# Conditioning units in the gaps of three norms, and the order of work around six norms, in a one-core decoder step

## What is computed

```
m = silu(c) @ W_ada + b_ada                 # per layer: 9 x 1024 outputs, for 9 conditioning vectors
shift1, scale1, gate1, shiftM, scaleM, gateM, shift2, scale2, gate2 = split(m, 9)
adaLN(x)  = rmsnorm(x) * g * (1 + scale) + shift
ffn(x)    = x + 0.5 * gate * ((silu(a) * b) @ W2),  a, b = split(adaLN(x) @ W1)
layer:  x = ffn1(x);  x = x + gateM * Mixer(adaLN(x));  x = ffn2(x)
```

## Time and profile before

| what | value |
|---|---|
| median of 3 runs | 1674.65 us (1674.52 to 1679.98) |
| profiled execution | 1671.24 us |
| its span in the trace | 1669.6 us (1.6 us lie around it) |
| PE busy | 1548.7 us (93%) |
| DVE, ACT, POOL busy | 871.4, 706.4, 252.2 us |
| granted PE clock, mean | 0.958 of full speed |

### The profile page before, as it was taken

The page is one execution under the profiler, slowest core; times in us unless marked ns, Lnnn a source line. Parts: engine busy times, 40 slices in busy tenths (PEclk is TensorE's granted clock), DMA queues, the critical chain, the costliest instruction groups (busy, mean ns, idle before and its releaser), DMA issues.

```text
span 1669.6 us, 32114 instructions
## 1 busy us (share of the span) xinstructions
PE 1548.7 (93%) x12092; PEld 1423.8 (85%) x12092; DVE 871.4 (52%) x1263; ACT 706.4 (42%) x896; POOL 252.2 (15%) x370
## 2 busy tenths in 40 slices
PE   5999999899899999899999899999988778899996
PEld 2899988887799998799999797899966557799996
DVE  1644443696644444544444632687457776644442
ACT  3433333432533333433333433566456784433332
POOL 2600000681400000100001101122230430100000
PEclk9899999999999999999999998899889898999998
DMA  9966678440676668776665552344571563654452
GB/s 294 262 226 226 210 253 271 144 131 15 192 248 220 219 221 267 230 239 221 222 186 155 159 160 63 89 114 125 218 240 52 173 202 122 194 184 159 146 165 87
DMA packets 269006, 304.80 MB, mean 183 GB/s; under 512 B 9945, under 2 KB 257857, under 8 KB 268792
## 3 DMA queue, kind: packets, MB, share of 16 engines
q1 hardware_dynamic: 260304, 274.96, 52.4%
q0 software_dynamic: 8624, 28.77, 5.3%
HBM read 300.51 MB, written 11.92 MB: 187 GB/s over the span
## 4 chain that ended last, share of the span: by engine, by line
PE 79%; DVE 6%; DMA 6%; ACT 6%; issue 2%; POOL 0%; SPq 0%; ACTq 0%; DVEq 0%; POOLq 0%
PE ps L2017 12%; PE ps L2018 11%; PE ps L2021 11%; PE ps L1998 7%; PE ps L1999 7%; PE ps L2000 7%; DMA raw<-in_ffn_w_dram 5%; PE ps L2031 3%; PE ps L2276 2%; PE ps L2278 2%; PE ps L2277 2%; PE ps L2254 2%; DVE wL L1304 2%; ACT wH L851 1%; PE ps L2117 1%
## 5 line engine op out<-in xcount | busy, mean ns | idle before, releaser
L1304 DVE TENSOR_TENSOR wL<-raw,wH 128x2048 fp32r<-128x2048 f32 (+2 forms) x176 | 366.7, 2083 | 392.7 <-ACT wH L851 392.5
L851 ACT ACTIVATE wH<-raw 128x2048 fp32r<-128x2048 f32 (+2 forms) x176 | 306.2, 1740 | 592.8 <-PE ps L2021 288.3
L1998 PE MATMUL ps<-hH,wL 128*128 128x288 f32 x848 | 260.9, 308 | 24.1 <-POOL hL L657 21.8
L2017 PE MATMUL ps<-hL,wH 128*128 128x288 f32 x976 | 267.5, 303 | 2.3 <-DVE hL L1920 1.8
L2018 PE MATMUL ps<-hH,wH 128*128 128x288 f32 x976 | 263.4, 296 | 0.0
L2000 PE MATMUL ps<-hH,wH 128*128 128x288 f32 x848 | 255.4, 301 | 0.0
L1999 PE MATMUL ps<-hL,wH 128*128 128x288 f32 x848 | 255.3, 301 | 0.0
L2017 PEld LDWEIGHTS ps<-hL,wH 128*128 128x128 f32 x976 | 184.3, 189 | 18.0 <-issue 16.0
L2017 PE MATMUL ps<-hidL,wH 128*128 128x288 f32 x704 | 194.7, 304 | 3.0 <-ACT wH L851 3.0
L2018 PE MATMUL ps<-hidH,wH 128*128 128x288 f32 x704 | 191.1, 297 | 0.0
L1998 PEld LDWEIGHTS ps<-hH,wL 128*128 128x128 f32 x848 | 165.1, 195 | 27.1 <-issue 24.3
(11 more groups left out here) (414 smaller groups left out, 2318.6 us busy)
## 6 DMA issues: line engine op xcount, KB each, us to landing
raw<-in_ffn_w_dram SPq DMA_DIRECT2D x88, 1024.0 KB, 5.2
ada<-in_ada_w_dram SPq DMA_DIRECT2D x72, 1024.0 KB, 5.2
raw<-in_ffn_w_dram SPq DMA_DIRECT2D x32, 768.0 KB, 4.7
raw<-in_ffn_w_dram SPq DMA_DIRECT2D x32, 640.0 KB, 5.3
craw<-in_cache_cmp_kv_dram SPq DMA_DIRECT2D x64, 256.0 KB, 3.6
raw<-in_nsa_w_in_dram SPq DMA_DIRECT2D x10, 1024.0 KB, 5.4
raw<-in_even_w_in_dram SPq DMA_DIRECT2D x8, 1024.0 KB, 5.5
kvp<-in_cache_sel_kv_dram POOLq DMA_DIRECT2D x64, 128.0 KB, 3.2
```

Source lines behind the costliest of these rows:

```text
L851: nc.scalar.activation(wH[parity][:, 0:k * UW], raw[parity][:, 0:k * UW], ACT.Copy).then_inc(hi_done, 1)
L1304: nc.vector.tensor_tensor(wL[parity][:, 0:k * UW], raw[parity][:, 0:k * UW], wH[parity][:, 0:k * UW].bitcast(F32), ALU.subtract).then_inc( ...
L1998: nc.tensor.matmul(o, l_, rhsH, start=first, stop=False)
L2017: nc.tensor.matmul(ps[:, banks + t, 0:T], wH[parity][:, c:c + P], L[:, k, :], start=first and k == k0, stop=False)
```

## The change

- Norms 2, 3 and 5 get two conditioning units each (32, 33; 56, 57; 68, 69), norm 0 keeps one (8). The first one of a pair is multiplied and turned in the gap, and finished by DVE after the norm's fourth chunk; the second one is multiplied right behind the turn. Its own turn comes in the first iteration of the W1 loop.
- The W1 loops have 11, 10, 10 and 2 units instead of 11, 11, 11 and 4. The turn of a unit comes one weight unit later than before: behind the next iteration's first unit, the last one behind the loop.
- SP sends both units of a norm between the first two loads of W1. In f = 3 it waits ahead of them for the last split of the attention output instead of the last output unit's end.
- The 2 MB of `w1c` go out in four pieces, each ahead of a quarter of W2.
- In every norm ACT rounds the sample columns first, ahead of chunk 0, without waiting for it.
- At the end of f = 0 and f = 2 DVE makes `wL` of the next stage's first unit ahead of the last update of x.
- The two loads of `c` move from POOL's queue to the head of SP's, and the constant fill no longer covers their rows.

```
-        ADA_IN_W1 = [9, 33, 57, 68]
-        ADA_PER_W1 = [HALF_PAIRS, HALF_PAIRS, HALF_PAIRS, 4]
+        ADA_IN_W1 = [9, 34, 58, 70]
+        ADA_PER_W1 = [HALF_PAIRS, HALF_PAIRS - 1, HALF_PAIRS - 1, 2]
+ADA_AT_NORM = [(8,), (), (32, 33), (56, 57), (), (68, 69)]
+        for pair in ADA_AT_NORM[2], ADA_AT_NORM[3], ADA_AT_NORM[5]:
+            ada_slot[pair[0]] = 1
...
 SP
+            sp.dma_start(rows[0:KD, 4, :], a["c_prompt"]...)          # from POOL, ahead of const
+            sp.dma_start(rows[KD:KD * NC, 4, :], a["c_sample"]...)
                 send(base, 0, w1v[f][:, :, 0:UW], KD)
-                if f < 3:
-                    send_one(a1 - 1)
+                if f == 3:
+                    sp.wait_ge(o_split, 3)
+                for n in ADA_AT_NORM[NORM_OF[f]]:
+                    send_one(n)
                 send(base + 1, 1, w1v[f][:, :, DFF:DFF + UW], KD)
-                if f == 3:
-                    sp.wait_ge(unit_used, OUT1 + 6)
                 send_one(a1)
...
                 if f == 2:
-                    quarter(0)
                     sp.wait_ge(ada_used, ADA_BY_NORM[4])
-                    for v in range(2):
-                        sp.dma_start(w1c[:, v, :, :], ...).then_inc(w1_landed, 16)
+                    for q in range(4):
+                        v, c = q // 2, q % 2 * 8
+                        sp.dma_start(w1c[:, v, c:c + 8, :], ...).then_inc(w1_landed, 16)
+                        quarter(q)
...
 POOL, norm
-                pool.wait_ge(hhi_done, 9 * k + 2)
+                pool.wait_ge(hhi_done, 9 * k + 1)
...
 ACT, norm
-                if ADA_AFTER_NORM[k] is not None:
-                    take_ada(ADA_AFTER_NORM[k])
+                if len(ADA_AT_NORM[k]) == 2:
+                    take_ada(ADA_AT_NORM[k][0])
+                act.wait_ge(ys_ready, 4 * k + 3)
+                nc.scalar.activation(hH[:, :, NP_:T], tmp[:, :, NP_:T], ACT.Copy).then_inc(hhi_done, 1)
                 for c in range(KD):
                     ...
-                    if c == 0:
-                        act.wait_ge(ys_ready, 4 * k + 3)
-                        nc.scalar.activation(hH[:, :, NP_:T], tmp[:, :, NP_:T], ACT.Copy).then_inc(hhi_done, 1)
+                if ADA_AT_NORM[k]:
+                    take_ada(ADA_AT_NORM[k][-1])
                 split(SECOND[k], 1)
...
 DVE, norm and ffn
-                    dve.wait_ge(hhi_done, 9 * k + (c + 2 if c else 1))
+                    dve.wait_ge(hhi_done, 9 * k + c + 2)
+                    if c == 3 and len(ADA_AT_NORM[k]) == 2:
+                        finish_ada(ADA_AT_NORM[k][0], link)
-                        finish_ada(a1 + j, ln)
+                        finish_ada(a1 + j - 1, ln)
+                finish_ada(a1 + ADA_PER_W1[f] - 1, link)
+                        if last and u == 2 and f in (0, 2):
+                            lower(n + 4, 0)
                         if u == (2 if last else 3):
                             pair_update(NORM_OF[f], q, bank, n + 3, ln)
-                        if not last or u < 2 or f < 3 and u == 2:
+                        if not last or u < 2 or f == 1 and u == 2:
...
 PE
+                for t, n in enumerate(ADA_AT_NORM[k]):
                     ada_unit(n, ada_slot[n], count[n])
-                    turn_ada(n)
+                    if t == 0 and len(ADA_AT_NORM[k]) == 2:
+                        turn_ada(n)
...
                     unit(na, 0, 0, 0, KD, hH, hL, True, True, NORM_OF[f])
                     if conditioned:
+                        turn_ada(a1 + j - 1)
                         ada_unit(a1 + j, 0, count[a1] + 16 * j)
                     pe.wait_ge(h_done, J + 1)
                     unit(na + 1, 1, 2, 0, KD, hH, hL, True, True)
-                    if conditioned:
-                        turn_ada(a1 + j)
+                turn_ada(a1 + ADA_PER_W1[f] - 1)                       # behind the loop
```

More of the change, by code:

```diff
@@ L485, in _ @@
         def _(sp):
+            sp.dma_start(rows[0:KD, 4, :], a["c_prompt"].rearrange("b (c p) -> (b c) p", p=P)).then_inc(c_landed, 16)
+            sp.dma_start(rows[KD:KD * NC, 4, :], a["c_sample"].rearrange("b (c p) -> (b c) p", p=P)).then_inc(c_landed, 16)
             sp.dma_start(const[:, :], a["consts"]).then_inc(const_landed, 16)
@@ L536, in ffn @@
                 if f == 2:
-                    quarter(0)
                     sp.wait_ge(ada_used, ADA_BY_NORM[4])
-                    for v in range(2):
-                        sp.dma_start(w1c[:, v, :, :], a["cmp_w1"][0, v].rearrange("(c p) h -> p c h", p=P)).then_inc(w1_landed, 16)
-                with sp.Fori(1 if f == 2 else 0, 4) as q:
-                    quarter(q)
+                    for q in range(4):
+                        v, c = q // 2, q % 2 * 8
+                        sp.dma_start(w1c[:, v, c:c + 8, :], a["cmp_w1"][0, v].rearrange("(c p) h -> p c h", p=P)[:, c:c + 8, :]).then_inc(w1_landed, 16)
+                        quarter(q)
+                else:
+                    with sp.Fori(0, 4) as q:
+                        quarter(q)
             def startup():
@@ L779, in _ @@
             pool.memset(cT[:, :, :], 0.0).then_inc(ones_ready, 1)
-            pool.memset(rows[:, :, :], 0.0).then_inc(ones_ready, 1)
+            pool.memset(rows[:, 0:4, :], 0.0).then_inc(ones_ready, 1)
             pool.wait_ge(ones_ready, 3)
-            pool.dma_start(rows[0:KD, 4, :], a["c_prompt"].rearrange("b (c p) -> (b c) p", p=P)).then_inc(c_landed, 16)
-            pool.dma_start(rows[KD:KD * NC, 4, :], a["c_sample"].rearrange("b (c p) -> (b c) p", p=P)).then_inc(c_landed, 16)
             flat = a["ada_b"].rearrange("l (c p) -> (l c) p", p=P)
@@ L1007, in odd @@
                 act.wait_ge(unit_used, OUT1 + 2)
-                act.wait_ge(w1_landed, 32)
+                act.wait_ge(w1_landed, 64)
                 for v in range(2):
@@ L1381, in norm @@
                     ins.then_inc(y_whole, 1)
-                if ADA_AFTER_NORM[k] is not None:
-                    finish_ada(ADA_AFTER_NORM[k], link)
             def ffn(f):
@@ L2058, in sum_squares @@
                 last_pair(k)
-                n = ADA_AFTER_NORM[k]
-                if n is not None and k > 0:
+                for t, n in enumerate(ADA_AT_NORM[k]):
                     ada_unit(n, ada_slot[n], count[n])
-                    turn_ada(n)
+                    if t == 0 and len(ADA_AT_NORM[k]) == 2:
+                        turn_ada(n)
             def ffn(f):
@@ L2224, in odd @@
                 pe.wait_ge(pe_copied, 1)
-                pe.wait_ge(w1_landed, 32)
+                pe.wait_ge(w1_landed, 64)
                 for v in range(2):
@@ L2643, in _ @@
                     pe.wait_ge(x_ready, KD)
-                    sum_squares(0, True)
+                    folded(0)
+                    last_pair(0)
             ada_unit(ADA_FIRST, ada_slot[ADA_FIRST], count[ADA_FIRST])
-            turn_ada(ADA_FIRST)
             ffn(0)
@@ L2692 @@
 SECOND = [1, IN0 + 1, FFN01 + 1, FFN10 + 1, IN1 + 1, FFN11 + 1]
-ADA_AFTER_NORM = [8, None, 32, 56, None, None]
+ADA_AT_NORM = [(8,), (), (32, 33), (56, 57), (), (68, 69)]
 _OUTS = [(1, 256, 1024), (8, 4, 1024), (1, 256, 1, 2, 4, 64), (8, 4, 1, 2, 4, 64), (1, 256, 1, 2, 4, 64), (8, 4, 1, 2, 4, 64),
```

## The result

The changed kernel takes 1687.7 us (median of 6 runs, 1685.94 to 1690.19), the kernel before 1674.6 beside it: a ratio of 1.0081 (95% interval 1.0064 to 1.0098). It is slower by 13 us, where 16.5 us of gain were forecast; the time lies above the range. The profiled execution took 1690.19 us, with a span of 1688.4, 18.8 longer than before.

The account below looks back on a forecast made before the run. PE was taken as the bound, busy 1548.7 of 1669.6 us. Terms -4.3 - 5.4 - 1.0 + 0.1 - 1.6 - 4.3 + 0 = -16.5 from the median 1674.65 gave 1658 us, range 1651 to 1667.

Parts of the forecast that it names:

- Units out of the W1 loops: W1 loops: fewer conditioning products and turns, moved turns wait for nothing; -4.28 us.
- the slower one: Rival, W1 loops: weights fall behind and conditioned iterations grow; 1684 at 1.2 us each; chance 0.05.
- the clock in the gaps: Gaps of norms 2, 3 and 5: second product keeps the clock at 1.00, low stretches go; -5.4 us.
- The clock falls anyway: Rival, gaps of norms 2, 3 and 5: clock drops all the same, 5.4 becomes 1.5; 1662; chance 0.20.
- the rival in which the clock stays up in norms 1 and 4 too: Shorter gaps there also keep the clock up, 2.1 + 1.7 us more gain; 1654.4; chance 0.08.
- The loops: W1 loops: iterations take 14.19 us with a conditioning unit and 12.77 without.
- ACT's order: Norms: samples rounded first start PE 0.5 us earlier; -1.0 counted in norms 1 and 4, +0.1 in norm 0.
- not under 15: Sign, norms: PE's wait for POOL's `hL` should fall from 21.8 us to under 15.
- the full doubling that the prediction weighed as its other end: Norms: DVE's first remainder doubles beside POOL; five starts 0.5 us later, sum 1.0 less.
- `lower` ahead of the update: Ends of f = 0 and f = 2: L1333 comes 0.87 and 0.7 us earlier; -1.57 together, at worst nothing.
- `w1c` in pieces: W2 of f = 2: PE's 2.98 us wait and its low-clock stretch go; -4.3 us, at the other end 0.
- The start: Program start: `c` earlier, other loads later; taken as 0, between -1.0 and +0.8; third unit not after 18.7.

Follow-up runs that it names:

- One: Changed kernel with one edit: in the W1 loops DVE finishes the previous iteration's conditioning unit ahead of `th`; 1661.3 us, ratio 0.9914.
- Four: One with the two loads of `c` back in POOL's queue; 1659.8 us, ratio 0.9911.
- Six: One with a single conditioning unit instead of two in norms 2 and 5, the pair kept in norm 3; 1662.5 us, ratio 0.9937.
- Three: Changed kernel with the two loads of `c` back in POOL's queue; 1691.9 us, ratio 1.0087.
- Seven: One with `w1c` whole again, in two loads of 1 MB behind the first quarter of W2; 1665.3 us, ratio 0.994.
- Ten: One with ACT's order in the norm undone, chunk 0 rounded ahead of the samples; 1660.5 us, ratio 0.992.
- Eleven: One with `lower` behind the last update of x again in f = 0 and f = 2; 1661.6 us, ratio 0.9923.
- Two: Kernel before with only the turns one weight unit later, and one conditioning unit in norm 5's gap; 1699.1 us, ratio 1.0143.
- Five: One with a single conditioning unit instead of two in each of norms 2, 3 and 5; 1671.3 us, ratio 0.9981.
- Eight: One with idle matmuls, whose results nothing reads, filling the gaps of norms 1 to 5; 1655.4 us, ratio 0.9875.
- Nine: Eight with the two loads of `c` back in POOL's queue; 1654.0 us, ratio 0.9886.

## Why the prediction was wrong

**The step that failed first** is "*Units out of the W1 loops*": "The moved turns wait for nothing: the copy and the bias of the unit before lie one weight unit back, some 6 us. DVE's `finish_ada` comes later by the same amount and runs as often." It was worked out for the middle of a loop and holds there, by only 1.36 us (586.40 to 587.76): DVE's chain behind a unit takes about 5 of the 6.4 us that it has. For the turn behind the loop there is no unit in between: the prediction counted these four turns, but gave them no wait. They wait 21.0 us, the clock behind them costs about 7.8, and both come back when the part alone is put into the kernel before. None of the rivals named it; the slower one (weights late in the W1 loops) did not happen: iterations run at the forecast pace.

**The step that failed second** is the clock in the gaps: "I take it that the clock stays at 1.00: the low stretches of these three norms go, 1.4 + 1.8 + 2.2 = 5.4 us." In after it fell in norms 2 and 3 and stayed up in norm 5; in the profiled execution of One it fell in all three. There the three stretches hold (0.27 + 0.45 + 0.44) x 2 x 6.4 = 14.8 us at the low level, where the earlier trace rows had 12.0, so in that execution the term is nothing. But one execution does not tell it. Seven kernels have two products in these gaps and nothing else to fill them. In norm 2 the mean clock of the first 6.4 us was 0.73 to 0.77 in all seven; in norm 3 it was 0.54 to 0.65 in six and 0.91 in Four (Six, with the pair in norm 3 alone, had 0.93); in norm 5 it was 1.00 in five and fell in two. Here is norm 5 in those not shown yet (Three, Four, Seven, Ten, Eleven), and then in the kernel before, with no product there, and in Six, with one:

```profile
1453.20:1459.60 6.40, 6.40 (x46) 6.16 (x47) 5.41 (x15) 4.36 (x8) 0.00 (x0) 1.00 1.01 325
1421.54:1427.94 6.40, 6.40 (x46) 6.16 (x47) 5.41 (x15) 4.36 (x8) 0.00 (x0) 1.00 0.98 325
1434.00:1440.40 6.40, 6.40 (x29) 6.40 (x30) 5.41 (x15) 4.35 (x8) 0.00 (x0) 0.55 1.00 324
1427.91:1434.31 6.40, 6.40 (x47) 6.22 (x48) 5.34 (x15) 4.42 (x8) 0.00 (x0) 1.00 0.97 321
1432.79:1439.19 6.40, 6.38 (x46) 6.14 (x47) 5.41 (x15) 4.35 (x8) 0.00 (x0) 1.00 0.98 312
...
1433.26:1439.66 6.40, 6.40 (x32) 6.40 (x33) 5.02 (x13) 4.78 (x7) 0.00 (x0) 0.62 0.01 4
1422.87:1429.27 6.40, 6.40 (x30) 6.40 (x31) 5.18 (x13) 4.38 (x8) 0.00 (x0) 0.59 0.54 173
```

With none or one product there (also 0.61 in Two and 0.54 in Five) it fell in all four. So of the 5.4 the 2.2 of norm 5 mostly came, the 1.4 of norm 2 never, the 1.8 of norm 3 hardly; that the second product is what holds norm 5 is likely from these eleven executions, and not shown by an edit of its own. The time is that of the rival "The clock falls anyway", 1662: without the fault of the loop ends the kernel takes 1661.3. Filled gaps hold the clock in all five norms, as Eight and Nine show. Their 1655.4 and 1654.0 lie near the 1654.4 of the rival in which the clock stays up in norms 1 and 4 too, but that rival had it from shorter gaps alone, which did not hold it.

**The loops** are as forecast. The turns in after's f = 1 follow each other by 14.19 to 14.20 us, and an iteration of f = 3 without a unit takes 12.76:

```profile
1498.99:1511.75 12.76, 12.76 (x98) 12.76 (x97) 6.01 (x4) 4.94 (x4) 0.00 (x0) 1.00 0.50 164
```

**ACT's order** gives 0.35 in place of 0.5, and PE's wait ends on DVE, as forecast; it is 17.4 us in all and not under 15, as norm 0 alone has 6.2 of it. What was mis-sized is DVE's first remainder beside POOL, here in after's norm 2, against the earlier trace rows:

```profile
450.88 0.73 POOL L663 TENSOR_TENSOR hL<-tmp,hH 128x256 fp32r<-128x256 f32 x1 [0.59 <-ACT hH L919]
...
451.23 0.65 DVE L1372 SCALAR_TENSOR_TENSOR hL<-tmp,adaT,hH 128x256 fp32r<-128x256 f32 x1 [0.27 <-ACT hH L922]
```

It takes 0.65 us beside POOL and 0.47 alone: 0.18, which by these rows is the missing part. The Trainium skill, GPSIMD Engine Reference, section Key points, says that POOL contends with DVE for the SBUF interfaces where DVE has two inputs there; the sign agrees, and the full doubling that the prediction weighed as its other end did not come. In norm 0 the loss is 0.34 against 0.1. Summed over norms 0, 1 and 4 that is -0.4, not -0.9: below what these runs can tell, as the tenth kernel shows.

**`lower` ahead of the update** gives 1.05 and 0.69, against 0.87 and 0.70: right in the trace, not to be told in the time.

**`w1c` in pieces**: the wait of 2.98 us is gone and 0.6 is PE's longest for `wH`; put back, it is 3.98 us and 4.0 us of time, against 4.3 forecast. Right in mechanism, and in size as far as the interval goes.

**The start** was taken at 0, up to +0.8. The third unit starts at 18.92, 1.07 after that of the earlier trace rows and past the 18.7 set as the limit:

```profile
18.92 1.94 PE L2039 MATMUL ps<-ada,cT 128*32 128x256 f32 x16 [0.16 <-DMA ada<-in_ada_w_dram]
```

That did not become time that can be measured: moved back, the loads of `c` gave nothing in three kernels. The first weight unit began at 52.06 in the ninth kernel, with `c` on POOL, and at 48.67 in the tenth, with `c` on SP. What makes the start differ by several us between executions stays open.

## What to carry to other kernels

When a step of a software pipeline is delayed by one stage, look at the loop's last pass by itself: inside the loop the next iteration's work covers the new dependence, behind the loop nothing does, and on an in-order engine all that follows stands behind the wait. On the engine that releases it, put the small operation that others wait for ahead of the one that itself waits. And do not count on a little work in a pause to hold TensorE's clock: see in the traces of several executions whether it holds, or fill the pause.

## What the runs showed of the hardware

In the norm-2 gap of after PE did a product (1.07 us), a turn and another product, with pauses of 2.00 us (ahead of the sum of squares), 1.72 and 1.19 us, and the granted clock was 0.50 in half of the next 6.4 us; with idle matmuls put into the last two of these pauses, and into the gaps of norms 1 and 4, it was 1.00 behind all five gaps of two kernels. The same gap can come out either way: norm 5, with the same work and a last pause of 1.19 us in both, had 1.00 in after and 0.56 in One, and 1.00 in five of seven executions. So one execution does not tell what a change does to the clock behind a gap, and the count of matmuls in a fixed stretch (29 to 37 against 46 to 48) shows it better than busy time, which is 100% in both.
